# The order of TensorE's half-height products in a two-block transformer kernel

## What is computed

```
# GLA: per head, A[t,s] = sum_k q[t,k] k[s,k] decay(t,s,k), causal; output A @ v, carried over chunks of 64 tokens
A = einsum('bhtk,bhsk,bhtsk->bhts', qi, ki, decay)
# DSA: an indexer scores all keys for each token and keeps the best 64
_, sel = top_k(score, topk)
logits = q . k[sel] * dh ** -0.5 + bias      # keys that were not chosen: -inf
p = softmax(logits)
```

## Time and profile before

| | |
|---|---|
| median of 3 runs | 1820.88 us (1820.84 to 1827.17) |
| the profiled execution | 1820.88 us |
| its span, first to last instruction | 1819.1 us |
| outside the span | 1.8 us |
| TensorE busy | 1782.6 us, 98% of the span |
| VectorE busy | 1361.2 us, 75% |
| ScalarE busy | 1141.9 us, 63% |
| mean granted TensorE clock | 0.993 |

### The profile page before, as it was taken

The page is one execution under the profiler, slowest core; times in us unless marked ns, Lnnn a source line. Parts: engine busy times, 40 slices in busy tenths (PEclk is TensorE's granted clock), DMA queues, the critical chain, the costliest instruction groups (busy, mean ns, idle before and its releaser), DMA issues.

```text
span 1819.1 us, 24797 instructions
## 1 busy us (share of the span) xinstructions
PE 1782.6 (98%) x9356; PEld 1492.4 (82%) x9356; DVE 1361.2 (75%) x1256; ACT 1141.9 (63%) x1153; POOL 126.2 (7%) x92
## 2 busy tenths in 40 slices
PE   9999999999999999999999999999999999889998
PEld 7888888888878888888888888888888879778886
DVE  3765655634478888888888888888888888965555
ACT  4655544544567777777777777777777763445453
POOL 0002000100041000000000000000000002110000
PEclk9999999999999999999999999999999999899999
DMA  9845555542479999999999999999999983335550
GB/s 287 270 137 165 187 192 191 167 139 93 152 275 374 393 364 393 358 382 390 351 392 369 373 389 352 394 382 358 394 366 374 395 303 128 116 105 187 189 190 35
DMA packets 255940, 502.57 MB, mean 276 GB/s; under 512 B 15004, under 2 KB 97493, under 8 KB 255502
## 3 DMA queue, kind: packets, MB, share of 16 engines
q1 hardware_dynamic: 248000, 474.67, 73.4%
q0 software_dynamic: 6976, 26.40, 4.7%
q10 hardware_dynamic: 910, 0.76, 0.1%
HBM read 493.90 MB, written 12.65 MB: 278 GB/s over the span
## 4 chain that ended last, share of the span: by engine, by line
PE 90%; DVE 5%; ACT 2%; POOL 1%; issue 1%; DMA 0%; DVEq 0%; POOLq 0%; SPq 0%; ACTq 0%
PE psum L585 24%; PE psum L587 23%; PE psum L588 23%; PE psum L794 9%; PE psum L796 5%; DVE psum L2156 1%; PE psum L1079 1%; PE psum L675 1%; ACT wh L1218 1%; PE psum L706 1%; POOL wl L2250 1%; DVE ta L2156 1%; DVE x L1701 1%; DVE wl L1637 1%; POOL rstd L2241 1%
## 5 line engine op out<-in xcount | busy, mean ns | idle before, releaser
L1637 DVE TENSOR_TENSOR wl<-ring,wh 128x2048 fp32r<-128x2048 f32 x443 | 1014.8, 2291 | 255.1 <-ACT wh L1218 252.0
L1218 ACT ACTIVATE wh<-ring 128x2048 fp32r<-128x2048 f32 x450 | 861.8, 1915 | 271.0 <-PE psum L585 169.3
L585 PE MATMUL psum<-wh,xT 128*128 128x512 f32 (+1 forms) x1136 | 431.4, 380 | 2.5 <-DVE wl L1637 1.1
L587 PE MATMUL psum<-wl,xT 128*128 128x512 f32 (+1 forms) x1136 | 424.4, 374 | 0.0
L588 PE MATMUL psum<-wh,xT 128*128 128x512 f32 (+1 forms) x1136 | 424.4, 374 | 0.0
L585 PE MATMUL psum<-wh,wnh 128*128 128x512 f32 x672 | 267.7, 398 | 1.5 <-DVE wnl L1793 1.5
L587 PE MATMUL psum<-wl,wnh 128*128 128x512 f32 x672 | 264.9, 394 | 0.0
L588 PE MATMUL psum<-wh,wnl 128*128 128x512 f32 x672 | 264.5, 394 | 0.0
L585 PEld LDWEIGHTS psum<-wh,xT 128*128 128x128 f32 x1136 | 214.2, 189 | 44.3 <-issue 3.0
L794 PE MATMUL psum<-xT,wh 128*128 128x512 f32 x704 | 249.5, 399 | 0.4 <-DVE xT L1647 0.4
L588 PEld LDWEIGHTS psum<-wh,xT 128*128 128x128 f32 x1136 | 214.0, 188 | 39.8
(11 more groups left out here) (296 smaller groups left out, 1398.6 us busy)
## 6 DMA issues: line engine op xcount, KB each, us to landing
ring<-in_w_moe SPq DMA_DIRECT2D x336, 1024.0 KB, 6.8
ring<-in_w_dense SPq DMA_DIRECT2D x33, 1024.0 KB, 5.2
ring<-in_w_in_ab SPq DMA_DIRECT2D x14, 1024.0 KB, 10.0
ring<-in_w_in_cd SPq DMA_DIRECT2D x12, 1024.0 KB, 5.3
ring<-in_w_gate SPq DMA_DIRECT2D x11, 1024.0 KB, 5.3
ring<-in_w_up SPq DMA_DIRECT2D x11, 1024.0 KB, 5.4
ring<-in_w_down SPq DMA_DIRECT2D x11, 1024.0 KB, 4.9
ring<-in_w_in SPq DMA_DIRECT2D x10, 1024.0 KB, 7.0
```

Of the source, the lines that this page charges most:

```text
L585: last = pe.matmul(o, a[0], b_[0], start=first, stop=False)
L587: pe.matmul(o, a[0], b_[1], start=False, stop=False)
L1218: act.activation(upper_half[i], ring[:, u_, :], ACT.Copy).then_inc(hi_ready[s_], 1)
L1637: dve.tensor_tensor(lower_half[i], ring[:, u_, :], upper_half[i].bitcast(F32), ALU.subtract)\
```

## The change

In `gla_products` the heads are no longer paired: all 8 matmuls of head 0 are issued, then all 8 of head 1, and so on, and within a head the 64-column matmuls stand in two places between the 128-column ones. In `group_scores` each head's mask matmul follows that head's score matmul directly, where before both scores came first and then both masks. The operands, the destinations, the number of matmuls and the semaphores are the same.

```diff
@@ group_scores @@
                     last = pe.matmul(o, q[rows, hp, t * P:(t + 1) * P], k[rows, hp, 0:n], start=True, stop=not (forget or masked))
                     first_of(last)
+                    if masked:
+                        last = pe.matmul(o, ident_r[:, :], keymask[:, t, 0:n], start=False, stop=True)
                     if forget:
                         last = pe.matmul(o, rowsel[:, 2 * hp + hh, :], nfT[:, 0:n], start=False, stop=True)
-                for hh in range(2 if masked else 0):
-                    last = pe.matmul(bank[hh][:, 0:n], ident_r[:, :], keymask[:, t, 0:n], start=False, stop=True)
                 last.then_inc(a_scores, 1)
@@ gla_products @@
-                def pieces(h):
+                for h in range(4):
                     r, c = slice(HD * (h % 2), HD * (h % 2) + HD), h // 2
                     b_ = bank[h]
-                    return ((b_[0:P, 0:64], gk[r, c, 0:P], gq[r, c, 0:64]),
-                            (b_[0:P, P:192], gko[r, c, 64:192], gqo[r, c, P:192]),
-                            (b_[0:P, 192:T], gko[r, c, 192:320], gqo[r, c, 192:T]),
-                            (b_[0:P, T:T + 64], gk[r, c, P:T], gq[r, c, P:192]),
-                            (b_[64:P, 64:P], gk[r, c, 64:P], gq[r, c, 64:P]),
-                            (b_[0:64, 64:P], gko[r, c, 0:64], gqo[r, c, 64:P]),
-                            (b_[64:P, T + 64:384], gk[r, c, 192:T], gq[r, c, 192:T]),
-                            (b_[0:64, T + 64:384], gko[r, c, 320:384], gqo[r, c, 192:T]))
-
-                for pair in ((0, 1), (2, 3)):
-                    for i in range(8):
-                        for h in pair:
-                            o, kk, qq = pieces(h)[i]
-                            last = pe.matmul(o, kk, qq, start=True, stop=True)
-                            first_of(last)
-                            if i == 7:
-                                last.then_inc(gla_A, 1)
+                    for o, m, kk, qq in (
+                        (b_[0:P, 0:64], P, gk[r, c, 0:P], gq[r, c, 0:64]),
+                        (b_[64:P, 64:P], 64, gk[r, c, 64:P], gq[r, c, 64:P]),
+                        (b_[0:64, 64:P], 64, gko[r, c, 0:64], gqo[r, c, 64:P]),
+                        (b_[0:P, P:192], P, gko[r, c, 64:192], gqo[r, c, P:192]),
+                        (b_[0:P, 192:T], P, gko[r, c, 192:320], gqo[r, c, 192:T]),
+                        (b_[0:P, T:T + 64], P, gk[r, c, P:T], gq[r, c, P:192]),
+                        (b_[64:P, T + 64:384], 64, gk[r, c, 192:T], gq[r, c, 192:T]),
+                        (b_[0:64, T + 64:384], 64, gko[r, c, 320:384], gqo[r, c, 192:T]),
+                    ):
+                        last = pe.matmul(o, kk, qq, start=True, stop=True)
+                        first_of(last)
+                    last.then_inc(gla_A, 1)
```

## The result

| | before | after |
|---|---|---|
| median | 1824.65 us (1820.84 to 1828.08, 12 runs) | 1834.49 us (1831.81 to 1840.64, 12 runs) |
| ratio | | 1.0056, 95% interval 1.0042 to 1.0069 |
| profiled execution, its span | 1820.88, 1819.1 us | 1832.02, 1830.2 us |

The changed kernel is slower by 0.56%, which on the median of before is 10.2 us (7.7 to 12.6). I had forecast 8.4 us, which lies inside that interval; the median of 1834.49 us lies 5.2 us above my 1829.3 and 1.5 us above my range. Of these 5.2 us, 3.8 are the base: over 12 runs the kernel before has a median of 1824.65 us, where I took 1820.88. In three later sets of runs it took 1821.17, 1822.88 and 1823.39 us. Both kernels vary by 7 to 9 us from run to run, which the experiments explain in part.

A forecast was written before the change was run, and what follows sets the result against it. TensorE, busy 98% of the span, was taken to bound the kernel. Products +3.9 us and scores +5.4, partly absorbed ahead of score group 4, gave +8.4 on 1820.9: 1829.3 us, range 1825.5 to 1833.0.

The forecast's parts named there:

- The products: `gla_products`: lost pairing and more changes of form make a head take 1.70 us, four 6.8 instead of 2.86; +3.9 us.
- The upper bound: `gla_products`: if the 64-column pairs were not side by side either, 0.9 us more, so +4.8 us.
- The scores: Masked score groups: three changes of form instead of one, four groups at +0.55 and four at +0.80; +5.4 us.
- the wait: TensorE's idle 1.33 us ahead of score group 4 absorbs part of the delay and shrinks to 0.4 us.
- Their sum: Whole kernel: 5.7 us of delay at score group 4 plus 2.7 from groups 4 to 7; +8.4 us.
- The clock: Products and following projection: the main forecast had no term for a fall in granted clock, leaving it to a rival.
- The base: Time of the kernel before, taken from its profiled execution, itself the median: 1820.9 us.
- Rival 1: Clock falls to half behind the products, 1.5 us per 3.42 us stretch; total 1830.8 to 1832.2 us; chance 0.36.
- Its argument against: Against a clock fall: TensorE also stood still 1.07 us in the third layer's longer half-clock stretch, never in the products.
- Rivals 2 and 3: Products and scores: other-row matmuls overtake queued ones, 1821 to 1823 us, chance 0.05; or switches are cheaper, 1824.7, chance 0.10.
- Rival 4: Third layer: clock falls move and two do not come, about -2.9 to -4.4 us; chance 0.02.
- The rule of the Trainium skill that I weighed: Products and scores: weight loads overlap matmuls only across different row groups; 0.8 and up to 1.7 us more, 1831.8; chance 0.04.

The follow-up runs named there:

- e5: Changed kernel, but products of heads 0 and 1 in gap 14, heads 2 and 3 in gap 15, half a projection between; 1834.86 us, ratio 1.007.
- e6: Changed kernel, plus each partner head's product made again on the other 64 rows into a bank nobody reads; 1831.2 us, ratio 1.0041.
- e2: Kernel before with only the new order of scores and masks in `group_scores`; 1826.56 us, ratio 1.0032.
- e1: Kernel before with only the new order of products in `gla_products`; 1830.61 us, ratio 1.0056.
- e4: Kernel before with heads one after another, but each head's four 128-column products first, then its four 64-column ones; 1829.44 us, ratio 1.0033.
- e8: Changed kernel run once more, unaltered, for a second profile; 1831.93 us in one run.
- e10: Kernel before with second-layer decay rows after both scores, and all heads' 128-column products ahead of the 64-column ones; 1815.69 us, ratio 0.9956.
- e9: Kernel before with both scores first, then both decay-row matmuls, in the second layer's eight `forget=True` groups; 1814.83 us against 1823.39, ratio 0.9956.

## Why the prediction was wrong

- **The products, +3.9 us: right.** A head takes 1.70 us at full clock, four take 6.8 in e5 and 6.9 in e6. The upper bound was added up wrong: a head has two such pairs of 64-column matmuls with two passes each, so it is 4 x 2 x 2 x 0.11 = 1.8, not 0.9. Nothing rests on it.
- **The scores, +5.4 us, less 1.0 in the wait: right.** e2 shows 4.4 net.
- **Their sum, +8.4 us: right as a sum of the order.** e5 and e6 show 8.5.
- **The clock, which the sum put at nothing: wrong.** This is the step of the mechanism that failed. The sum priced 6.8 us of products on half of the rows, and the projection behind them, by spacings at 2.4 GHz, and gave the clock no term. The clock fell in all four profiles in which the products ran on one half of the rows at a time in one piece (changed, e1, e4, e8) and at this place in none of the others. In the stretch it cost 12.7 - 8.5 = 4.2 us (10.2 us of lower clock) or 11.2 - 8.5 = 2.7 (6.8 us), 0.4 us for each microsecond.
- **The base, 1820.9 us: too low by 3.8.** This is most of the miss in the number. I took the median of three runs, though one of them was 1827.17, and set the forecast and the top of the range from it. By the ratio the change is +10.2 us, which on my base would be 1831.1, inside the range. The falls of the clock that come and go spread both kernels: of 21 executions of before beside e1 to e4, the fastest (1818.69 us) has a mean clock of 0.994 and the slowest (1826.72) one of 0.989.
- **Rival 1 came true**, at a chance of 0.36. It had the change at 9.9 to 11.3 us, and +10.2 was measured. Its price, 1.5 us for each 3.4, was right (e10). What was mis-sized is how many: two or three such lengths in the profiles, where it counted one or two. Its argument against, that the stretches at half clock also had idle time, was no argument: TensorE had none here.
- **Rivals 2 and 3: refuted.** In these traces TensorE takes nothing out of order from the other rows, and a head on the other 64 rows still starts only 0.07 us before the last one's end (88.86 against 88.71 + 0.22).
- **Rival 4 did not come.** The changed kernel lacks the fall near 1550 us, and what lies behind the layer norm is 0.2 us shorter, not 1.5.
- **The rule of the Trainium skill that I weighed (TensorE: Matmul & The Clock Gate, "The mechanism") did not hold here**, and there were rows I had overlooked. By it a head would take 1.90 us; it takes 1.70. I wrote that no alternation within one row group stands in the trace; the `forget` groups of before come close, with 64-row scores and 8-row matmuls in turn. One score takes 0.42 us up to the next form there (390.94 - 390.52), the number of my sum, not 0.53.

## What to carry to other kernels

In these traces, matmuls that contract over 64 channels shared the array's time only if neighbours in the program lay in different row groups, and each change between the forms 64*128 and 64*64 cost about 0.15 us. Put heads in pairs, put all that has one form together, and look for every place where a mask or bias matmul stands between the two heads of a pair: moving such matmuls out from between the heads in the second layer (e9) gave 0.44% here. When an edit thins out TensorE's work for several microseconds, count the clock as a cost of its own, even if the engine never idles.

## What the runs showed of the hardware that I had not expected

- The granted clock fell to 0.5 with TensorE busy all the time, in the midst of products on 64 of the 128 rows. With the same holes and the other 64 rows filled (e6) it stayed at 1.00, and with 3.0 us of dense matmuls between two thin pieces of 3.4 us (e5) too, each in one profile.
- 32 more products cost 0.1 us (6.93 against the 6.8 of the sum), since they ran beside the others, and in this stretch the kept clock saved 2.7 us or more.
- Each microsecond at the lower clock made the stretch 0.4 us longer (4.2 us for 10.2, 2.7 for 6.8, 1.5 for 3.4). A fall ahead of the program's last one lasted 3.4, 6.8 or 10.2 us.
